# The product with the values one place earlier: order of TensorE's work in two attention stages

## What is computed

```
h = rms_norm(x, ln1_g);  proj = h @ w_in
o_a = mla_mixer(...)      # per head: softmax(q k^T + mask) v
o_b = nsa_mixer(...)      # sum over 3 branches of gate * softmax(q k^T + bias) v
mix = concat(rms_norm(o_a), rms_norm(o_b))
x = x + mix @ w_o
x = x + square(relu(rms_norm(x) @ w_up)) @ w_down
```

## Time and profile before

| | us |
|---|---|
| median of three executions | 746.54 |
| profiled execution | 745.74 |
| its span, first to last instruction | 743.7 |
| TensorE busy in the span | 698.9 |
| VectorE busy | 366.8 |
| ScalarE busy | 291.8 |
| GpSimd busy | 103.5 |
| mean granted TensorE clock | 0.982 |

### The profile page before, as it was taken

One profiled execution on the slowest core, in us unless ns is written; L12 is line 12 of the kernel. 1 busy time (PEld: TensorE's weight loads), 2 busy tenths in 40 slices (PEclk: granted clock), 3 DMA queues, 4 the chain that ended last, 5 costly groups with the idle time before them and its releaser, 6 DMA issues.

```text
span 743.7 us, 9977 instructions
## 1 busy us (share of the span) xinstructions
PE 698.9 (94%) x3703; PEld 595.9 (80%) x3703; DVE 366.8 (49%) x713; ACT 291.8 (39%) x630; POOL 103.5 (14%) x152
## 2 busy tenths in 40 slices
PE   7995989999989789979799999999999999999998
PEld 5984768888879778868679888888888888888886
DVE  5557556546696653575675544412324454532311
ACT  5564545346485342354534434321122433422110
POOL 2444642310050300223110000000000000000000
PEclk9999899999999979999999999999999999999999
DMA  7341133111053100010003332232322323232302
GB/s 273 124 143 46 43 94 107 33 57 30 4 159 123 57 1 1 2 58 28 29 28 115 114 100 99 87 112 85 114 85 92 106 85 113 85 114 85 100 1 99
DMA packets 17953, 60.04 MB, mean 81 GB/s; under 512 B 2120, under 2 KB 2248, under 8 KB 17906
## 3 DMA queue, kind: packets, MB, share of 16 engines
q1 hardware_dynamic: 16562, 55.41, 22.4%
q0 software_dynamic: 1200, 3.94, 1.7%
q10 hardware_dynamic: 144, 0.07, 0.0%
HBM read 57.26 MB, written 2.15 MB: 80 GB/s over the span
## 4 chain that ended last, share of the span: by engine, by line
PE 84%; DVE 7%; ACT 3%; issue 3%; POOL 1%; DMA 1%; SPq 0%; DVEq 0%; ACTq 0%; POOLq 0%
PE bank L1397 14%; PE bank L1399 14%; PE bank L1398 14%; PE bank L1695 8%; PE bank L1697 8%; PE bank L1696 8%; PE bank L1418 6%; PE bank L1581 5%; PE bank L1544 2%; PE bank L1623 1%; DVE w_lo L906 1%; ACT p_buf L720 1%; PE bank L1555 1%; DVE s_buf L1062 1%; DMA x<-x 1%
## 5 line engine op out<-in xcount | busy, mean ns | idle before, releaser
L906 DVE TENSOR_TENSOR w_lo<-raw,w_hi 128x1024 fp32r<-128x1024 f32 (+3 forms) x97 | 112.5, 1166 | 128.6 <-ACT w_hi L598 128.4
L598 ACT ACTIVATE w_hi<-raw 128x1024 fp32r<-128x1024 f32 (+3 forms) x97 | 97.4, 1011 | 120.2 <-PE bank L1399 118.2
L1695 PE MATMUL bank<-act_hi,w_hi 128*128 128x512 f32 (+3 forms) x288 | 106.9, 371 | 0.0
L1697 PE MATMUL bank<-act_hi,w_lo 128*128 128x512 f32 (+3 forms) x288 | 106.8, 371 | 0.0
L1696 PE MATMUL bank<-act_lo,w_hi 128*128 128x512 f32 (+3 forms) x288 | 106.8, 371 | 0.0
L1397 PE MATMUL bank<-w_hi,a_hi 128*128 128x512 f32 x256 | 99.7, 389 | 0.0
L1399 PE MATMUL bank<-w_hi,a_lo 128*128 128x512 f32 x256 | 99.7, 389 | 0.0
L1398 PE MATMUL bank<-w_lo,a_hi 128*128 128x512 f32 x256 | 99.7, 389 | 0.0
L1397 PE MATMUL bank<-w_hi,act_hi 128*128 128x512 f32 (+3 forms) x224 | 92.4, 413 | 2.3 <-DVE act_lo L919 2.3
L1399 PE MATMUL bank<-w_hi,act_lo 128*128 128x512 f32 (+3 forms) x224 | 81.6, 364 | 0.0
L1398 PE MATMUL bank<-w_lo,act_hi 128*128 128x512 f32 (+3 forms) x224 | 81.4, 363 | 0.0
(11 more groups left out here) (192 smaller groups left out, 1086.9 us busy)
## 6 DMA issues: line engine op xcount, KB each, us to landing
raw<-weights SPq DMA_DIRECT2D x86, 512.0 KB, 3.3
raw<-weights SPq DMA_DIRECT2D x7, 384.0 KB, 4.4
x<-x SPq DMA_DIRECT2D x4, 512.0 KB, 6.5
bias<-bias_by_distance POOLq DMA_DIRECT2D x1, 2048.0 KB, 9.5
y<-x SPq DMA_DIRECT2D x8, 256.0 KB, 2.2
raw<-weights SPq DMA_DIRECT2D x4, 288.0 KB, 2.8
raw<-weights SPq DMA_DIRECT2D x4, 280.0 KB, 3.1
consts<-consts SPq DMA_DIRECT2D x1, 688.0 KB, 4.2
```

The costliest lines, as they stand in the source:

```text
L598: act.activation(w_hi[:, m % RING, 0:width], raw[:, n % RAW, 0:width], ACT.Copy).then_inc(*hi_done.mark(n))
L906: dve.tensor_tensor(w_lo[:, m % RING, 0:width], raw[:, n % RAW, 0:width], w_hi[:, m % RING, 0:width].bitcast(F32), ALU.subtract).then_inc( ...
L1695: pe.matmul(dst, h[:, ws], act_hi[:, k, cols], start=k == 0, stop=False)
L1697: ins = pe.matmul(dst, l[:, ws], act_hi[:, k, cols], start=False, stop=k == KD - 1)
```

## The change

In both loops over n the call of mix_unit(n - 4) stands ahead of turn_unit(n - 2). Everything else keeps its place: what each call issues, its waits and its semaphores, and all other engines' lists.

```
@@ MLA loop
                 if n in TURN_AT:
                     turn_heads(*TURN_AT[n])
+                if n - 4 >= 0:
+                    mix_unit(n - 4)
                 if n - 2 >= 0 and n - 2 < N_MLA:
                     turn_unit(n - 2)
-                if n - 4 >= 0:
-                    mix_unit(n - 4)
                 if n - 4 in ROW_END[0:8]:
                     turn_nsa(ROWS[ROW_END.index(n - 4)])
@@ NSA loop
                 compress(n - N_MLA)
+                if n - 4 >= N_MLA and n - 4 < last:
+                    mix_unit(n - 4)
                 if n - 2 >= N_MLA and n - 2 < last:
                     turn_unit(n - 2)
-                if n - 4 >= N_MLA and n - 4 < last:
-                    mix_unit(n - 4)
                 if n - 9 >= N_MLA and n - 9 < last and UNITS[n - 9][0] == "cmp":
                     turn_mix(1, UNITS[n - 9][1])
```

## The result

Over four runs each the changed kernel took 738.09 us in the median (737.65 to 741.91 us) and the kernel before 747.82 us (746.1 to 750.01 us): a ratio of 0.9886 (95%: 0.986 to 0.9913), 9.7 us less. A later set of runs gave 737.33 against 747.07 us, 0.9863 (0.9842 to 0.9884). The forecast was 741.6 us with a range from 739.3 us, so the sign was right and the size too small by 3.5 us.

The account below looks back on a forecast made before the run. TensorE, 84% of the chain, was taken as the bound, with gains only where it idles. Filled waits of 3.2 us plus 1.7 us of clock made 4.9 us, forecasting 741.6 us, range 739.3 to 745.4 us.

Parts of the forecast that it names:

- Filled waits, 3.2 us: TensorE's waits at the turns of a unit: products run inside them, gaining 3.2 us in five terms.
- (a) to (c): Steps 54, 56, 60: product fills waits for kc_row, v_diag, k_cmp, gaining 1.14, 0.79, 0.60 us.
- (d): Products behind the waits of 1.07 and 1.56 us, two records each, move inside them: 0.40 us together.
- (e): Near 312.7 us: a wait of 0.34 us is filled by the product, gaining 0.30 us.
- Nothing from 319 to 335 us: Waits at turns and a product there: no gain counted, savings return as longer waits; bounds 0 and 0.65 us.
- The later exponentials: ScalarE's exponentials wait for turns ending one product later: cost between 0 and 9.7 us, taken as nothing.
- products wait for pt_buf in number: Sign that the forecast is wrong: many products on TensorE waiting for their pt_buf copy; no size given.
- the slower rival: Later exponentials decide, at odd units on ScalarE behind L1418: 7.2 us cost less 3.2 us, 750.5 us; chance 0.07.
- The steady state, "nothing to win": Steps without waits: turns 0.44 us, product 0.81 us, next scores follow at once, so no gain.
- The clock behind the wait for v_diag, 1.7 us: From 268 to 274 us the clock is 0.72; the shorter wait was taken to spare that stretch, 1.7 us.
- The clock at 361 us: From 360 to 366 us the clock is 0.72; with 1.4 us idle left, no gain was counted.
- both stretches: Rival: full clock both behind the v_diag wait and at 360 to 366 us, 739.9 us; chance 0.08.

Follow-up runs that it names:

- the twelve steps alone: Kernel before with the product first only in the twelve steps where TensorE waited at the turns: 742.54 us, ratio 0.9937.
- steps 54 to 60: Kernel before with the product ahead of the turns in steps 54, 56, 59 and 60 only: 745.05 us, ratio 0.9966.
- NSA alone: Kernel before with the new order in the NSA loop only: 743.01 us, ratio 0.993.
- its two variants: Changed kernel with the first w1 job one step later, 738.1 us; changed kernel with step 78 put back to turns first, 737.95 us.
- four steps alone: Kernel before with the product ahead in steps 89, 93, 94 and 96 only: 745.23 us, ratio 0.9981.
- The other steps alone: Kernel before with the product first in all steps but the twelve with waits: 748.72 us; the same with the first w1 job a step later: 748.11 us.

## Why the prediction fell short

**Filled waits, 3.2 us: right.** For (a) to (c) I had 2.53 us; the idle time from 54 to 61 fell from 7.44 to 5.12 us, 2.3 us, and v_diag and k_cmp kept 1.03 and 0.56 us for the 1.2 and 0.6 us worked out. (d), 0.40 us, stands against 0.6 us of idle time. (e) at 312.7 us was 0.36 us for 0.30. That these gains are those of the product inside the wait is shown by the twelve steps alone.

**Nothing from 319 to 335 us: right.** 28.67 for 28.78 us. What the product saved at 322 us came back as the wait of 3.21 us, and the turns behind that wait cost nothing.

**The later exponentials, taken as nothing: right for the whole change.** The waits of L720 for L1418 grew from 11.2 us at 12 places to 28.4 at 20 (second trace of the changed kernel), and the only waits for p_buf left on TensorE, 1.2 us, are shorter than before. My sign "products wait for pt_buf in number" came in a small way, 2.2 us in two places: 0.94 us at the end of MLA, where the stretch is shorter all the same, and 1.2 us near 360 us, where the turns come no later. I found no place where the slower rival decides.

**The steady state, "nothing to win": wrong.** This is the step that failed outright. I read from the earlier trace rows that each operation follows the last at once, and took a hand-over without idle time for one without cost. The pair turns, product before scores is 0.05 us longer than product, turns. With all but the twelve steps turned, that gave 1.1 us in MLA, 0.5 from 42 to 54 and 0.4 from 61 to 77, of which 0.3 us were lost again at the taps. There TensorE waits for tap_planes, a chain of VectorE: 1.16 us at the second place for 0.67 before. With the wait in MLA that got shorter, the sum is 1.6 us from the stretches of MLA, taps and w1 (1.30 - 0.29 + 0.58) and about 0.4 us more behind them.

**The clock behind the wait for v_diag, 1.7 us: right for the whole change, but these steps alone don't bring it.** The kernel before has two stretches of the lower clock there, one around the end of the wait for kc_row and one behind v_diag, which is the one that I priced. Windows of before (the clock is the last but two of the numbers):

```profile
259.00:266.00 7.00, 5.98 (x29) 6.01 (x29) 2.47 (x9) 3.71 (x9) 0.72 (x2) 0.51 0.01 2
269.00:273.00 4.00, 4.00 (x23) 3.90 (x21) 1.99 (x5) 1.79 (x6) 0.00 (x0) 0.57 0.00 0
```

In the changed kernel's first trace the clock is 1.00 behind kc_row's stretch, which is as long as before:

```profile
262.00:269.20 7.20, 6.04 (x28) 6.07 (x29) 3.60 (x11) 3.87 (x9) 0.73 (x2) 0.53 0.01 2
269.20:280.50 11.30, 9.70 (x69) 8.64 (x68) 8.58 (x27) 5.33 (x15) 0.00 (x0) 1.00 0.00 0
```

So the stretch that I named has gone, and from 54 to 61 this trace is 4.35 us shorter, for the 2.53 + 1.7 us of the sum. In the second trace the other stretch is halved as well:

```profile
261.00:265.00 4.00, 4.00 (x23) 3.98 (x22) 2.18 (x7) 3.50 (x8) 0.15 (x1) 0.57 0.02 4
```

That makes 1.2 us more (busy time 15.73 for 16.94 us), which differs between two traces of one kernel. The cause that I gave, the shorter wait for v_diag, is not shown: in the traces of the twelve steps, of steps 54 to 60 and of NSA alone this wait is shortened too (1.42, 0.73 and 0.73 us), and the clock behind it is low all the same. Over the seven traces with the product ahead there the clock from 54 to 61 ran from 0.62 to 0.92, over the seven without from 0.69 to 0.86. The four of the whole change and its two variants lie at 0.84 to 0.92; why they lie at the good end was not settled, so for this term the number may be luck. The Trainium skill, page "TensorE: Matmul & The Clock Gate", section "Why this matters for your kernels", warns of idle gaps longer than any of these but the one for kc_row. The wait of 1.56 us near 360 us, with a stretch of the lower clock behind it until these steps were turned, speaks against that as the only cause.

**The clock at 361 us, "I leave that one": wrong.** It was the rival "both stretches", at 0.08. It went in seven of seven traces, and four steps alone bring it. The busy time there fell by 1.2 us. I had seen that 1.4 us of idle time would be left and had rows on either side; the runs put 1.18 us, with 0.4 us of work behind it, with the spared ones.

**The sum.** 4.9 us predicted; the second traces differ by 9.8 us. The two terms that I put at nothing measured 2.0 us (hand-overs and the wait in MLA) and 1.2 us (the clock at 361 us). The clock from 54 to 61 gave 3.0 us for 1.7, of which 1.2 us is in one of two traces only. That makes 4.5 of the 4.9 us missed; the rest is within the size of the terms. That the median of before, 747 us in later sets, was higher than the 746.54 us I began from is 0.5 us of the miss of the ratio, not of the time.

**Open.** What places the stretches of the lower clock. The other steps alone save 1.7 us by their steady steps and ran 1.8 and 1.0 us above before in the median, with intervals that include no change. Their runs have a lower mean clock (0.976 and 0.975 for 0.979), which fits the loss; a trace of theirs shows the clock at 0.69 from 54 to 61 and a stretch of the lower clock behind the waits at 337 us instead of among them. For the same reason it is open why the whole change has more of the full clock than its parts.

## What to carry over

An engine that is never idle in a timeline can still lose time where one kind of work hands over to the next: take the time from step to step with the same work in either order (here 0.25 and 0.30 us for the same two matmuls), since 0.05 us in some 40 steps is more than any single wait filled here. When filling waits, count TensorE's clock with each of them by the busy time of the same matmuls, and look where the lower clock lies: while other engines set the time it only shortens a wait. Expect that part to vary by kernel and by run, so that the medians of partial edits need not add up to that of the whole. Cut traces at the same instruction and compare stretch by stretch before explaining a total.

## What the runs showed of the hardware

- A product of 128x64 matmuls directly ahead of the scores makes these 0.05 us longer (0.30 for 0.25 us), in each MLA step of before that has no other turns between; a single 128x128 transpose between them removes it. It is not known whether the weight load of the scores is what is late. In before the scores' first load starts 0.06 us ahead of their first matmul where the product stands ahead (129.36 and 129.42 us), and 0.11 us where turns do (132.01 and 132.12 us), but no run changed the loads alone.
- The lower clock, 1.2 GHz, costs by its place: the same 3.4 us of it left the stretch from 77 to 89 at 28.7 us when it lay among waits and at 30.3 us when it lay behind them, since between the waits the turns start 6.8 us behind the product at either clock.
- With steps 89, 93, 94 and 96 turned, the wait of 1.56 us near 360 us became 1.18 us of idle time and 0.4 us of work, and the clock stayed at 1.00 to the last scores, in seven traces of seven. Without, it was about 0.89 over that stretch, in seven of seven.
- The granted clock from 54 to 61 differed between two traces of one kernel (0.84 and 0.92) with the same idle time, 5.07 and 5.12 us.
